# Attention steps between the products of a decoder layer: scores of the next row tile moved behind the values, transposed probabilities moved one eighth of the products later

## The reference, cut to what matters

```python
h = rmsnorm(x, norm1_g)
xa, ga, q, k, v, gate_a, gate_b = split(h @ w_in)
branch_a = (rg_lru(conv(xa)) * gelu(ga)) @ w_br_a
q, k = rmsnorm(q, q_norm_g), rmsnorm(k, k_norm_g)
for g, (window, dilation) in enumerate(((128, 1), (512, 4), (2048, 16))):
    # 4 heads of 128 per group; per query at most window // dilation + 1 keys
    s = where(valid, (q[g] . k[g][pos - offs]) * 128 ** -0.5, -1e30)
    m = max(s); p = exp(s - m); den = sum(p)
    o[g] = (p . v[g][pos - offs]) / den;  lse[g] = m + log(den)
att = sum(softmax(lse over g) * o)
branch_b = att @ w_br_b
x = x + (sigmoid(gate_a) * branch_a + sigmoid(gate_b) * branch_b) @ w_out
x = x + (gelu(gf) * vf) @ w_down       # [gf, vf] = conv(rmsnorm(x) @ w_up)
```

## Time and profile before

| | us |
|---|---|
| median of 3 runs | 1185.78 |
| lowest and highest run | 1184.78, 1185.96 |
| profiled execution, its own time | 1185.64 |
| span of its trace | 1183.9 |
| TensorE busy in the span | 1177.8 (99%) |
| TensorE weight loads busy | 1138.4 (96%) |
| VectorE, ScalarE, GpSimd busy | 652.6 (55%), 459.4 (39%), 173.4 (15%) |

### The profile page before, as it was taken

One profiled execution on the slowest core, in us unless ns is written; L12 is line 12 of the kernel. 1 busy time (PEld: TensorE's weight loads), 2 busy tenths in 40 slices (PEclk: granted clock), 3 DMA queues, 4 the chain that ended last, 5 costly groups with the idle time before them and its releaser, 6 DMA issues.

```text
span 1183.9 us, 21737 instructions
## 1 busy us (share of the span) xinstructions
PE 1177.8 (99%) x9049; PEld 1138.4 (96%) x9049; DVE 652.6 (55%) x1328; ACT 459.4 (39%) x723; POOL 173.4 (15%) x273
## 2 busy tenths in 40 slices
PE   9999999999999999999999999999999999999998
PEld 7998998998999999999999999999999999999998
DVE  6553543533622255666645458888337884378731
ACT  6443444444433357667533444222212222122231
POOL 2265144152240000000100120000100001000010
PEclk9999999999999999999999999999999999999999
DMA  8576346255332222231262232232323323232232
GB/s 239 133 210 166 91 125 162 78 142 146 95 104 59 72 83 79 72 89 55 78 180 79 70 89 83 78 89 74 92 73 87 88 72 94 72 89 75 85 97 61
DMA packets 183781, 118.52 MB, mean 100 GB/s; under 512 B 7379, under 2 KB 175975, under 8 KB 183687
## 3 DMA queue, kind: packets, MB, share of 16 engines
q1 hardware_dynamic: 172352, 89.47, 26.9%
q0 software_dynamic: 11344, 28.01, 8.7%
q10 hardware_dynamic: 10, 0.01, 0.0%
HBM read 107.43 MB, written 8.45 MB: 98 GB/s over the span
## 4 chain that ended last, share of the span: by engine, by line
PE 99%; DVE 1%; ACT 0%; issue 0%; ACTq 0%; DVEq 0%
PE ps L658 66%; PE ps L637 20%; PE ps L964 2%; PE ps L728 1%; PE ps L715 1%; PE ps L792 1%; PE ps L877 1%; PE ps L796 1%; PE ps L756 1%; PE ps L771 1%; PE ps L740 1%; PE ps L802 1%; PE ps L759 1%; PE ps L940 0%; PE ps L680 0%; DVE w_s L1448 0%
## 5 line engine op out<-in xcount | busy, mean ns | idle before, releaser
L658 PE MATMUL ps<-h,w_s 128*128 128x288 f32 x3840 | 517.6, 296 | 0.0
L658 PEld LDWEIGHTS ps<-h,w_s 128*128 128x128 f32 x3840 | 512.7, 189 | 4.7 <-issue 4.7
L1442 DVE TENSOR_TENSOR w_s<-w_raw,w_s 128x1024 fp32r<-128x1024 f32 (+1 forms) x160 | 193.9, 1212 | 189.1 <-ACT w_s L1050 189.0
L1050 ACT ACTIVATE w_s<-w_raw 128x1024 fp32r<-128x1024 f32 (+1 forms) x160 | 166.2, 1039 | 330.7 <-PE ps L658 326.4
L637 PE MATMUL ps<-w_s,h 128*128 128x384 f32 x1152 | 218.1, 341 | 0.9 <-DVE w_s L1448 0.5
L637 PEld LDWEIGHTS ps<-w_s,h 128*128 128x128 f32 x1152 | 198.5, 188 | 4.8 <-issue 2.4
L658 PE MATMUL ps<-g_hi,w_s 128*128 128x288 f32 x672 | 119.2, 297 | 0.0
L658 PEld LDWEIGHTS ps<-g_hi,w_s 128*128 128x128 f32 x672 | 99.3, 189 | 0.0
L658 PE MATMUL ps<-g_lo,w_s 128*128 128x288 f32 x336 | 72.0, 296 | 0.0
L599 POOL DMA_DIRECT2D out<-f_row x12 | 6.2, 520 | 416.6 <-ACT f_row L1396 416.6
L658 PEld LDWEIGHTS ps<-g_lo,w_s 128*128 128x128 f32 x336 | 54.1, 189 | 0.0
(11 more groups left out here) (299 smaller groups left out, 1453.8 us busy)
## 6 DMA issues: line engine op xcount, KB each, us to landing
w_raw<-in_w_in SPq DMA_DIRECT2D x65, 512.0 KB, 4.0
w_raw<-in_w_up SPq DMA_DIRECT2D x48, 512.0 KB, 4.0
w_raw<-in_w_down SPq DMA_DIRECT2D x24, 512.0 KB, 3.7
kc<-in_cache_k_g POOLq DMA_DIRECT2D x48, 128.0 KB, 3.2
vc<-in_cache_v_g POOLq DMA_DIRECT2D x12, 512.0 KB, 6.1
w_raw<-in_w_out SPq DMA_DIRECT2D x8, 512.0 KB, 3.7
w_raw<-in_w_br_a SPq DMA_DIRECT2D x7, 512.0 KB, 3.7
x_tok<-in_x_prompt SPq DMA_DIRECT2D x4, 512.0 KB, 7.6
```

What stands on the lines that cost most here:

```text
L658: last = mm(pu[u % 2][:, 512 * a:512 * a + HALF], w[:, part, k, :], x[:, k, HALF * a:HALF * (a + 1)], start=(k == 0 and i == 0), stop=(k = ...
L1050: A(w_s[:, ring(u), 0, 0:nkt[u], :], w_raw[:, u % NRAW, 0:nkt[u], :], ACT.Copy).then_inc(hi_ready, 1)
L1442: TT(w_s[:, ring(u), 1, 0:nkt[u], :], w_raw[:, u % NRAW, 0:nkt[u], :], w_s[:, ring(u), 0, 0:nkt[u], :], ALU.subtract).then_inc(lo_ready, 1)
```

## The change

The table `NEXT_PE` moves S1 to S4 from the front of a tile (k = 0, directly behind P) to k = 4, directly behind V. P1 to P4, O0 to O2 and O4 move from k = 0 to k = 1, three products later (six in a gate unit), and O3 from k = 2 to k = 1, directly behind P4. P0 stays where it is. On VectorE the mask and maximum of the next scores now stand behind the split of the weights. On ScalarE, in the gate units of the last head, the exponential now stands behind the copy of the gate product (`gate_raw`).

```diff
-NEXT_PE = {0: {1: "B0"}, 1: {0: "P0 S1", 4: "V0"}, 2: {0: "P1 S2 O0", 4: "V1"}, 3: {0: "P2 S3 O1", 4: "V2"},
-           4: {0: "P3 S4 O2", 4: "V3"}, 5: {0: "P4", 2: "O3", 4: "V4"}, 6: {0: "O4"}}
+NEXT_PE = {0: {1: "B0"}, 1: {0: "P0", 4: "V0 S1"}, 2: {1: "P1 O0", 4: "V1 S2"}, 3: {1: "P2 O1", 4: "V2 S3"},
+           4: {1: "P3 O2", 4: "V3 S4"}, 5: {1: "P4 O3", 4: "V4"}, 6: {1: "O4"}}
@@ ScalarE, gate units of the last head
+                if m:
+                    gate_raw(U_GA + m - 1, sg_a[:, m - 1, :])
                 if m < 5:
                     exps(NH - 1, m)
-                if m:
-                    gate_raw(U_GA + m - 1, sg_a[:, m - 1, :])
@@ VectorE, row tiles
-                    if prev and s < 5:
-                        mask_max(hp - 1, s)
                     if s == 7:
                         middle_features(hp, 0)
                         sample_keys(hp)
                     split_ahead(hp, s)
+                    if prev and s < 5:
+                        mask_max(hp - 1, s)
@@ VectorE, gate units
+                if m:
+                    lo_split(U_GA + m + 1)
                 if m < 5:
                     mask_max(NH - 1, m)
-                if m:
-                    lo_split(U_GA + m + 1)
```

## The result

| | median, us | ratio to before | 95% interval |
|---|---|---|---|
| before (6 runs) | 1186.10 | | |
| with the change (6 runs) | 1196.36 | 1.0090 | 1.0079 to 1.0100 |

The change costs 10.3 us; 9.1 had been forecast. The profiled execution took 1195.97 us.

A forecast was written before the change was run, and what follows sets the result against it. TensorE's own stream was taken to bound the kernel. Joins -6.9, O's wait +15.7 and softmax +0.3 made +9.1 us, taking the profiled 1185.64 to 1194.7 and, with the median 0.1 above, 1195 us; range 1188.5 to 1202.

The forecast's parts named there:

- The bound: TensorE, busy 1177.8 of 1183.9 us, bounds the kernel; any wait added to its stream is paid in full.
- O behind P: TensorE, O0 to O3: each waits for ScalarE's copy of the P just ahead, 16 x 0.98 = +15.7 us.
- S behind V: TensorE, V and S joined, P and O touching: idle gaps around 32-column strips go, -6.9 us.
- The softmax: Way from S to P: less time, short by about 0.1 us at P4 of three heads, +0.3 us.
- Rival 1: Softmax chain late as well, P late by 0.6 us at 12 places: +7 us, 1202 us; chance 0.12.
- (a): TensorE's waits list O for ScalarE's copy 16 times, about 0.9 us each; busy time drops by about that.
- (b): Between V and S no idle weight loads; V's strips to S's first take 0.37 us instead of 0.57.
- Rival 2: TensorE: avoided changes at V and S outweigh O's wait, not slower, 1184.6 or 1178.8 us; chance 0.09.
- Rival 3: TensorE's clock falls to the 1.2 GHz level after the gaps: +18 us on top, 1213 us; chance 0.03.

The follow-up runs named there:

- experiment 1: Changed kernel without O's wait (pT_ready) for ScalarE's copy of the transposed probabilities; 1180.38 us, ratio 0.9952 to the kernel before.
- experiment 5: Changed kernel with ScalarE's copy behind P1 to P4 lengthened by an extra 256-column copy before pT_ready; 1199.98 us, ratio 1.0120 to the kernel before.
- experiment 2: Kernel before the change, without O's wait (pT_ready) for ScalarE's copy of the transposed probabilities; 1185.08 us, ratio 0.9993.
- experiment 4: Changed kernel with S ahead of V instead of behind it, at the same places; 1201.33 us, ratio 1.0128 to the kernel before.

## Why the prediction was right

- **The bound.** It held that a wait put into TensorE's stream is paid in full. 16 waits of 0.96 us account for 15.4 us, and without them the kernel is 16.0 us faster in the medians and 15.2 in the spans (1194.2 to 1179.0, experiment 1). A longer copy was felt in full within the heads (experiment 5).
- **O behind P** (forecast +15.7). It came to +15.4: the copy started 0.63 us behind P in the row tile too (forecast 0.64), and O's load 0.11 behind the copy's end (0.12). What hid the copy before was S at 12 of the 16 places. At O3, two blocks of products hid it, which the prediction did not set apart. It changes nothing in the sum.
- **S behind V** (forecast -6.9). This term was sized too large. It is 0.39 instead of 0.45 us per row tile: V's first strip to S's first took 0.46 and not 0.37, while S itself took 1.01 and not 1.04. The first strip of S has its load at 196.04 and its product only at 196.15. In the last head it is 0.31. There the last scores to the products behind O took 0.25 us before (363.73 to 363.98), in a row tile 0.34 (190.53 to 190.87): 0.09 of the 0.45 was the rest of O's wait, which experiment 2 takes away. S1 gave 0.28 and not 0.37. By the row tile's starts: 9 x 0.39 + 3 x 0.31 + 4 x 0.28 = 5.6. Experiment 1 against the kernel before is -5.5. That the gain comes from the order of V and S is shown by experiment 4.
- **The softmax** (forecast 0.1 at three P4). It waits at exactly three places. The order in time, P4 after:

```profile
214.27 0.42 PEld L771 LDWEIGHTS ps<-const,prob 128*128 128x128 f32 x4 [0.29 <-ACT prob L1154]
```

  The load came 2.29 us behind S4's last start (211.98), forecast 2.26. The weight loads lose 0.29 us, but in other tiles they run ahead of the transposes by 0.18, so the path loses 0.1. Rival 1, the chain late throughout, did not occur: in row tile 2 VectorE's split ended at 196.20, and the mask began at 197.45 with 1.24 us of idle time between (forecast: 1 us of cover).
- **The sum.** 15.4 - 5.6 + 0.3 = 10.1 of the 10.3 us in the spans, and the first head was reached 0.18 us later than before (91.59 against 91.41 at L745). Of the 1.2 us by which the forecast was low, the joins make 1.3, and the wait takes back 0.3.
- **Two of its signs failed.** (a) expected the busy time to drop by about as much as O waits, and it dropped by 2.1 us. The idle time did grow by 12.4 us (6.1 to 18.5), the wait's 12.5, but some 3 us of the 15.4 lost count as busy, while the 5.6 us that the joins save came out of busy time. (b) expected 0.37 us from V's strips to S's, and it took 0.46.
- **Rival 2** (not slower) needed the 0.41 us ahead of L759 to go, and they stay (6.6 us at 16 places before and after). **Rival 3**: the granted clock is 1.00 in the profile after, in the tile with the wait and over the span. Sixteen gaps of 0.8 to 1 us, 7 to 10 us apart within a head, did not lower it. The rule on short idles (the Trainium skill, TensorE: Matmul & The Clock Gate, A second HAM failure mode) describes another outcome, which no run here shows.

The wait itself orders nothing here. O writes columns 896 to 1023 of `TRN` and the copy reads columns 0 to 511, and O waits for its operand and for its target by `o_ready` and `at_ready`. Why it was written is not to be seen from the kernel.

## What to carry to other kernels

When a step is moved away, ask what it covered: here the scores, at one of four places two blocks of products, stood between transposes and a step that waits for their copy, and without them the wait was open at 16 places. A gain in the engine's own stream (strips behind strips) and a loss by a wait are independent, and can be had apart. Removing the wait that no data need turned +10.3 us into -5.5. On an engine that is busy for 99% of the time such a sum can be made from start times, place by place; here it came within 1.2 us.

## What the runs showed of the hardware

- TensorE's weight loads stood idle at most changes between full-width weights and 32-column strips. Ahead of strips it was 0.17 us behind full-width transposes, and behind full-width products 0.25 (384 columns) or 0.17 (288; experiment 4, last head, 379.11). Behind strips it was 0.20 where these multiply 128 columns and 0.41 where they multiply 256. From V's strips to S's there was no idle time, but the first product of S came 0.11 us behind its load. Within V, from full width (L792) to strips (L796), none is listed either, though the kind changes there.
- From the end of ScalarE's copy to the waiting weight load on TensorE took 0.11 us (193.29 to 193.40). One wait cost more than these two together: 0.96 us per place, for a copy of 0.60.
